# The seam between two layers: the sample tile first, and two chunks of the next layer between the last transposes

## What is computed

```
o = concat(ya, yb) @ w_out_even          # 2048 -> 1024
x1 = x + rmsnorm(o, g_post)
```

```
h = rmsnorm(x1, g_pre)
q, k, v, z, f = split(h @ w_in_odd)      # 4 x 1024 and 8 columns
logf = log_sigmoid(f + b_forget)         # then a running sum over all keys, also over 256 cached rows
```

## Time and profile before

| | |
|---|---|
| median of 3 runs | 1696.01 us |
| the profiled execution | 1696.7 us, its span 1694.9 us |
| TensorE matmuls (PE) busy | 1587.4 us, 94% |
| VectorE (DVE) busy | 809.8 us, 48% |
| ScalarE (ACT) busy | 669.2 us, 39% |
| POOL busy | 440.1 us, 26% |
| mean granted clock of TensorE | 0.976 |

### The profile page before, as it was taken

The page is one execution under the profiler, slowest core; times in us unless marked ns, Lnnn a source line. Parts: engine busy times, 40 slices in busy tenths (PEclk is TensorE's granted clock), DMA queues, the critical chain, the costliest instruction groups (busy, mean ns, idle before and its releaser), DMA issues.

```text
span 1694.9 us, 26649 instructions
## 1 busy us (share of the span) xinstructions
PE 1587.4 (94%) x9562; PEld 1462.9 (86%) x9562; DVE 809.8 (48%) x1753; ACT 669.2 (39%) x1243; POOL 440.1 (26%) x267
## 2 busy tenths in 40 slices
PE   5899999998999999999997999999999999995798
PEld 5899999998998999888886998889889898884576
DVE  5755677664883321336565543443434433342332
ACT  6433333332233332335454344545445445542221
POOL 1113453343212121244442212221213122232000
PEclk9999999999999999999998999999999999997899
DMA  4121213112102111154554444723323342222122
GB/s 143 39 65 56 67 56 97 55 43 67 50 13 66 38 49 37 58 178 150 172 190 88 77 60 42 70 40 63 56 41 70 43 69 41 68 68 75 38 82 75
DMA packets 128740, 121.06 MB, mean 71 GB/s; under 512 B 9706, under 2 KB 112500, under 8 KB 128684
## 3 DMA queue, kind: packets, MB, share of 16 engines
q1 hardware_dynamic: 128684, 120.30, 29.1%
HBM read 101.61 MB, written 18.66 MB: 71 GB/s over the span
## 4 chain that ended last, share of the span: by engine, by line
PE 79%; issue 6%; DVE 6%; ACT 5%; POOL 1%; DMA 1%; SPq 0%; POOLq 0%; ACTq 0%; DVEq 0%
PE PB L720 74%; PE PB L724 5%; DVE NRML L1737 2%; POOL WOL L698 1%; ACT L1239 1%; ACT L1629 1%; ACT SB L1701 1%; ACT WH L1233 0%; DMA XS<-in_x_prompt_dram 0%; ACT NRMH L1233 0%; DMA nf_rows<-NFROW 0%; ACT PT L1233 0%; DVE DTROW L1737 0%; POOL WL L604 0%; DVE XT L1744 0%
## 5 line engine op out<-in xcount | busy, mean ns | idle before, releaser
L720 PE MATMUL PB<-HH,WH 128*128 128x352 f32 x1872 | 620.9, 332 | 14.6 <-ACT XR L1253 6.0
L720 PE MATMUL PB<-HH,WL 128*128 128x352 f32 x1872 | 605.0, 323 | 0.0
L720 PE MATMUL PB<-HL,WH 128*128 128x352 f32 x1872 | 604.4, 323 | 0.0
L720 PEld LDWEIGHTS PB<-HH,WH 128*128 128x128 f32 x1872 | 355.2, 190 | 28.7 <-issue 20.4
L720 PEld LDWEIGHTS PB<-HL,WH 128*128 128x128 f32 x1872 | 355.8, 190 | 0.0
L720 PEld LDWEIGHTS PB<-HH,WL 128*128 128x128 f32 x1872 | 354.5, 189 | 0.0
L604 POOL TENSOR_TENSOR WL<-WRAW,WH 128x1024 fp32r<-128x1024 f32 x82 | 200.5, 2446 | 565.3 <-ACT WH L1233 550.0
L1233 ACT ACTIVATE WH<-WRAW 128x1024 fp32r<-128x1024 f32 x112 | 117.7, 1052 | 26.6 <-DMA WRAW<-in_w_in_even_dram 19.3
L1737 DVE TENSOR_TENSOR Y<-PB,Y 128x128 f32 (+2 forms) x72 | 20.2, 281 | 163.8 <-PE PB L720 163.8
L1701 ACT ACTIVATE SB<-SB,small 128x128 f32<-128x128 f32 (+8 forms) x72 | 53.8, 748 | 81.3 <-DVE small L1741 81.3
L720 PE MATMUL PB<-PT,VTOK 128*128 128x128 f32 (+2 forms) x624 | 82.2, 275 | 0.0
(11 more groups left out here) (290 smaller groups left out, 2453.0 us busy)
## 6 DMA issues: line engine op xcount, KB each, us to landing
WRAW<-in_w_out_even_dram SPq DMA_DIRECT2D x48, 512.0 KB, 3.5
WRAW<-in_w_in_even_dram SPq DMA_DIRECT2D x44, 512.0 KB, 3.8
WRAW<-in_w_in_odd_dram SPq DMA_DIRECT2D x32, 512.0 KB, 8.3
ACSB<-acs_rows SPq DMA_DIRECT2D x16, 528.0 KB, 4.8
NFB<-nf_rows SPq DMA_DIRECT2D x8, 656.0 KB, 3.9
XS<-in_x_prompt_dram SPq DMA_DIRECT2D x8, 512.0 KB, 6.0
XT<-in_x_prompt_dram SPq DMA_DIRECT2D x8, 512.0 KB, 4.8
x_rows<-OG SPq DMA_DIRECT2D x8, 512.0 KB, 5.3
```

Of the source, the lines that this page charges most:

```text
L720: return pe.matmul(out, lhsT, rhs, start=start, stop=stop)
```

## The change

The sample tile is treated first in the closing pass and in the steps behind it: `place` gives the new position of a tile (SMP 6, tile 6 7, tile 7 8), and waits count by it. The interleaving of these steps on ScalarE and VectorE is written out anew. Behind the transposes of tile 6 TensorE does V0 and V1, then the transposes of tile 7, and after F2 goes on with V2. POOL splits the V weights ahead of its wait for `h1_lo` 17. The reads of F0 and F1 on ScalarE stand between the tiles' steps. The transposes of the forget row go from behind Z1 (step 4) to behind Q0 (step 6). The diff, cut to its core:

```diff
+    def place(t):
+        return 6 if t == SMP else t + 1 if t >= 6 else t
+    def h_turns(t):
+        return 2 * t + 2 if t < 6 else 13 if t == SMP else 2 * t + 3
...
 @sync
         def x1_out(b):
-            sp.wait_ge(S("x1"), b + 1)
+            sp.wait_ge(S("x1"), place(b) + 1)
...
-        for b in (6, 7, SMP):
+        for b in (SMP, 6, 7):
             x1_out(b)
         sp.wait_ge(S("h1_lo"), 17)
-        for b in (6, 7, SMP):
+        for b in (SMP, 6, 7):
             sp.wait_ge(S(x1_stored(b)[0]), x1_stored(b)[1])
...
 @gpsimd
         split_low(tile_no(W_F, 1, 0))
+        split_low(tile_no(W_QKVZ + V_, 4, 0))
         pool.wait_ge(S("h1_lo"), 17)
...
-        split_low(tile_no(W_QKVZ + V_, 4, 0))
         split_low(tile_no(W_QKVZ + Z_, 4, 0))
...
 @tensor
-            pair = (2, 3) if b < 3 else (0, 1) if b < 6 else ((4, 5), (6, 7))[b - 6]
+            pair = (2, 3) if b < 3 else (0, 1) if b < 6 else ((2, 3), (4, 5))[b - 6]
...
-        for j, t in enumerate(tiles):
+        for j, t in ((2, SMP), (0, 6), (1, 7)):
             out_step(t, 46, j)
             out_step(t, 47, j).then_inc(S("p_chunk"), 2)
...
         project_chunk(w_f, u_f, 0, HH, HL)
         project_chunk(w_f, u_f, 1, HH, HL)
+        pe.wait_ge(S("o_g"), 14)
+        turn_h1(SMP)
         pe.wait_ge(S("o_g"), 16)
-        pe.wait_ge(S("o_sq"), 16)
         turn_h1(6)
+        project_chunk(w_v, u_v, 0, HH, HL)
+        project_chunk(w_v, u_v, 1, HH, HL)
         pe.wait_ge(S("o_g"), 18)
-        pe.wait_ge(S("o_sq"), 18)
         turn_h1(7)
-        turn_h1(SMP)
         pe.wait_ge(S("h1_lo"), 17)
         project_chunk(w_f, u_f, 2, HH, HL)
...
             for i in range(STEPS):
-                if project:
+                if project and (attend or i >= 2):
                     j = i // 3
                     project_chunk(...)
...
-                if not attend and i == 4:
+                if not attend and i == 6:
                     turn_lrow()
...
 @scalar
+        def read_f(c):
+            act.wait_ge(S("p_chunk"), 3 * W_F + (1, 2, 5)[c])
+            copy(FW[0][:, c * CH:(c + 1) * CH], PB[c][0:HEADS_C, 0:CH]).then_inc(S(f"c_read{c}"), 1)
+        squares(SMP)
+        squares_sample()
         squares(6)
+        root(SMP)
         root(6)
         squares(7)
+        split_high(tile_no(W_QKVZ, 1, 0))
+        squares_x1(SMP)
         squares_x1(6)
+        root_x1(SMP)
+        read_f(0)
         root(7)
-        squares(SMP)
-        split_high(tile_no(W_QKVZ, 1, 0))
         root_x1(6)
+        h1_high(SMP)
         squares_x1(7)
-        squares_sample()
+        read_f(1)
         h1_high(6)
         root_x1(7)
-        root(SMP)
-        squares_x1(SMP)
         h1_high(7)
-        root_x1(SMP)
-        h1_high(SMP)
-        read_chunks(tile_no(W_F, 1, 0), whole(FW[0], HEADS_C), rows=HEADS_C)
+        read_f(2)
         split_high(tile_no(W_F + 2, 1, 0))
         log1p_exp_steps(...)
...
 @vector
+        gained(SMP)
         gained(6)
+        mean(SMP)
         mean(6)
+        residual(SMP)
         gained(7)
         mean(7)
         residual(6)
-        gained(SMP)
-        mean_x1(6)
-        residual(7)
-        normed_x1(6)
-        mean(SMP)
-        mean_x1(7)
-        normed_x1(7)
-        residual(SMP)
-        h1_low(6)
         mean_x1(SMP)
         normed_x1(SMP)
+        residual(7)
+        mean_x1(6)
+        normed_x1(6)
+        h1_low(SMP)
+        mean_x1(7)
+        h1_low(6)
+        normed_x1(7)
         h1_low(7)
-        h1_low(SMP)
```

More of the change, by code:

```diff
@@ L962, in turn_h1 @@
             src = XTT[2 if b == SMP else b % 2]
-            pe.wait_ge(S("xn1"), b + 1)
+            pe.wait_ge(S("xn1"), place(b) + 1)
             if b == SMP:
@@ L1012, in _ @@
         u_f = tile_no(W_F - OE_UNITS, 1, 0)
+        w_v = tile_no(W_QKVZ + V_, 4, 0)
+        u_v = tile_no(W_QKVZ - OE_UNITS + V_, 4, 0)
         pe.wait_ge(S("h1_lo"), 12)
@@ L1152, in turn_steps @@
             for i in range(STEPS):
-                if project:
+                if project and (attend or i >= 2):
                     j = i // 3
                     project_chunk(tile_no(W_QKVZ + j, 4, p), tile_no(W_QKVZ - OE_UNITS + j, 4, p), i % 3, HH, HL)
-                else:
+                if not project:
                     if i == 0:
@@ L1460, in squares @@
             for c in range(2):
-                act.wait_ge(S("p_chunk"), 3 * (W_OE + 16 * (t // 3) + 15) + t % 3 + 1 if t < 6 else 273 + 2 * (t - 5))
+                act.wait_ge(S("p_chunk"), 3 * (W_OE + 16 * (t // 3) + 15) + t % 3 + 1 if t < 6 else 3 * (W_OE + 46) + 2 * (place(t) - 5))
                 bank = PB[PAIRS[t % 4][c]]
@@ L1465, in squares @@
                 else:
-                    wait(act, "o_sq", 2 * t + c)
+                    wait(act, "o_sq", 2 * place(t) + c)
+                    if t == 6:
+                        act.wait_ge(S("s_sq"), 1)
                     act.activation(JUNK[:, c * HALF:(c + 1) * HALF], bank[:, :], ACT.Square,
@@ L1477, in root @@
             rows = sample_rows(t)
-            act.wait_ge(S("o_ms"), t + 1)
+            act.wait_ge(S("o_ms"), place(t) + 1)
             row_root(ORR[0:rows, t:t + 1], OSA[0:rows, t:t + 1], "o_rt")
@@ L1483, in squares_x1 @@
             src = OGT[2 if t == SMP else t % 2]
[L1484 to L1488, removed]
+            act.wait_ge(S("x1"), place(t) + 1)
+            wait(act, "x1_sq", place(t))
+            act.wait_ge(S("o_sq"), 6 * (t // 3) + 4 + 2 * (t % 3 == 2) if t < 6 else 18)
             act.activation(JUNK[0:rows, :], src[0:rows, :], ACT.Square, accum_out=OSX[0:rows, t:t + 1]) \
@@ L1493, in root_x1 @@
             rows = sample_rows(t)
-            act.wait_ge(S("x1_ms"), t + 1)
+            act.wait_ge(S("x1_ms"), place(t) + 1)
             row_root(OSX[0:rows, t:t + 1], OSX[0:rows, t:t + 1], "x1_rt")
@@ L1498, in h1_high @@
             if t == SMP:
-                act.wait_ge(S("h_turn"), 17)
-                copy(HH[:, :, SEQ:TOK], PB[3][:, 0:KT * DEC].rearrange("p (k l) -> p k l", l=DEC)).then_inc(S("h1_hi"), 1)
+                act.wait_ge(S("h_turn"), h_turns(t))
+                copy(HH[:, :, SEQ:TOK], PB[6][:, 0:KT * DEC].rearrange("p (k l) -> p k l", l=DEC)).then_inc(S("h1_hi"), 1)
                 return
-            pair = (2, 3) if t < 3 else (0, 1) if t < 6 else ((4, 5), (6, 7))[t - 6]
+            pair = (2, 3) if t < 3 else (0, 1) if t < 6 else ((2, 3), (4, 5))[t - 6]
             for c in range(2):
-                act.wait_ge(S("h_turn"), 2 * t + c + 1)
+                act.wait_ge(S("h_turn"), h_turns(t) - 1 + c)
                 copy(HH[:, 4 * c:4 * c + 4, t * P:(t + 1) * P],
@@ L2038, in gained @@
                 bank = PB[PAIRS[t % 4][c]]
-                dve.wait_ge(S("o_sq"), 2 * t + c + 1)
+                dve.wait_ge(S("o_sq"), 2 * place(t) + c + 1)
                 if t == SMP:
@@ L2051, in mean @@
                 return
-            dve.wait_ge(S("o_sq"), 2 * t + 2)
+            dve.wait_ge(S("o_sq"), 2 * place(t) + 2)
             ts(OSA[:, t:t + 1], OSA[:, t:t + 1], OSB[:, t:t + 1], D * EPS, ALU.add, ALU.add).then_inc(S("o_ms"), 1)
@@ L2057, in residual @@
             at_ = 2 if t == SMP else t % 2
-            dve.wait_ge(S("o_rt"), t + 1)
+            dve.wait_ge(S("o_rt"), place(t) + 1)
             dve.wait_ge(S(f"x_in{t}"), 32)
             order.fence()
-            dve.wait_ge(S("o_g"), 2 * t + 2)
+            dve.wait_ge(S("o_g"), 2 * place(t) + 2)
             stt(OGT[at_][0:rows, :], OGT[at_][0:rows, :], ORR[0:rows, t:t + 1], XTT[at_][0:rows, :], ALU.mult, ALU.add) \
@@ L2066, in mean_x1 @@
             rows = sample_rows(t)
-            dve.wait_ge(S("x1_sq"), t + 1)
+            dve.wait_ge(S("x1_sq"), place(t) + 1)
             ts(OSX[0:rows, t:t + 1], OSX[0:rows, t:t + 1], D * EPS, None, ALU.add).then_inc(S("x1_ms"), 1)
@@ L2072, in normed_x1 @@
             at_ = 2 if t == SMP else t % 2
-            dve.wait_ge(S("x1_rt"), t + 1)
-            dve.wait_ge(S("x1"), t + 1)
+            dve.wait_ge(S("x1_rt"), place(t) + 1)
+            dve.wait_ge(S("x1"), place(t) + 1)
             stt(XTT[at_][0:rows, :], OGT[at_][0:rows, :], OSX[0:rows, t:t + 1], PREB[0:rows, :], ALU.mult, ALU.mult) \
@@ L2079, in h1_low @@
             if t == SMP:
-                dve.wait_ge(S("h1_hi"), 17)
-                tt(HL[:, :, SEQ:TOK], PB[3][:, 0:KT * DEC].rearrange("p (k l) -> p k l", l=DEC),
+                dve.wait_ge(S("h1_hi"), h_turns(t))
+                tt(HL[:, :, SEQ:TOK], PB[6][:, 0:KT * DEC].rearrange("p (k l) -> p k l", l=DEC),
                    HH[:, :, SEQ:TOK].bitcast(f32), ALU.subtract).then_inc(S("h1_lo"), 1)
                 return
-            pair = (2, 3) if t < 3 else (0, 1) if t < 6 else ((4, 5), (6, 7))[t - 6]
+            pair = (2, 3) if t < 3 else (0, 1) if t < 6 else ((2, 3), (4, 5))[t - 6]
             for c in range(2):
-                dve.wait_ge(S("h1_hi"), 2 * t + c + 1)
+                dve.wait_ge(S("h1_hi"), h_turns(t) - 1 + c)
```

6 lines of the change are left out of this document (3 added, 3 removed).

## The result

The changed kernel takes 1703.6 us (median of 6 runs, 1703.1 to 1705.0); the kernel before takes 1697.3 us in the same comparison (6 runs, 1694.9 to 1699.0). The ratio is 1.0039, 95% interval 1.0029 to 1.0049: slower by 0.4%, with the whole interval beyond the 0.2% (3.4 us) that the prediction took as the least difference a measurement of this kernel can tell. The forecast was 1704.8, range 1698.5 to 1709.5.

What follows compares the result with a forecast made beforehand. The prediction took TensorE, busy 94% of the span, as the bound. Z0 +4.8, half clock in Z0 +2.5 and forget row +1.5 gave +8.8 us: 1705.5 profiled, 1704.8 as median, range 1698.5 to 1709.5.

Steps and rivals of the forecast that it cites:

- the seam: Stretch between the two layers: 8.2 us of TensorE standing still and 2.5 us of half clock, all the change can win.
- T: Moment the last transposed tile is split; 925.4 before, forecast 929.7, or 932.2 with V0 at half clock.
- Z0: First Z chunk, waiting for V0's bank to be read: start at T + 16.3, 948.5 against 943.69, +4.8 us.
- V0's half clock: V0, after a stretch with only short transposes, runs at half clock: 2.5 us, bound 0.
- The tie: POOL's low split of V against VectorE's residual of tile 6, ready within 0.1 us; VectorE taken to go first.
- Rival 3: POOL goes first ahead of VectorE's residual of tile 6: +1.75 us, 1706.6 us; chance 17%.
- Half clock in Z0: Z0 runs at half speed behind TensorE's gap of 8.4 us: +2.5 us, bound 0.
- Forget row: Its transposes move from after Z1 to after Q0, delaying the store of the running sums: +1.5 us.
- Norm sum: Gap ahead of TensorE's first norm sum grows from 1.86 to 3.3 us; possible half clock, 0 to 1.8, left out.
- the list of what would show it: Last transposes at 927 to 930, gap 6 to 9 us ahead of Z0, store 6 to 10 us later.
- Rival 1: Seam filled, V0 read before TensorE finishes V2, Z0 directly behind V2: 1694 us, or 1691.5; chance 8%.
- Rivals 2 and 4: 2: chain to T shorter, 1698.9 us, 12%. 4: V0 runs only after tile 7's transposes, about 1707 us, 4%.

Runs made afterwards that it cites:

- e2: Changed kernel with ScalarE's reads of V0 and V1 moved ahead of the read of F2; 1699.6 us, ratio 1.0011.
- e11: Changed kernel with the store of the running sums issued as soon as they are ready; 1700.9 us, ratio 1.0018.
- e3: Changed kernel with the early Z load and the early reads of V0 and V1; 1699.8 us, ratio 1.0009.
- e9: Changed kernel with early Z load, early reads of V0 and V1, and running sums stored first; 1689.0 us, ratio 0.9952.
- e10: Same edits to the changed kernel as e9, plus tile 7's transposes between V0 and V1; 1690.6 us, ratio 0.9961.
- e1: Changed kernel with SyncE's Z load of head 0 issued early, no longer waiting for T; 1703.3 us, ratio 1.0032.
- e7: Kernel before with the Z load of head 0 issued early, nothing else; 1697.9 us, ratio 1.0000.
- e8: Kernel before with the store of the running sums issued as soon as they are ready; 1693.1 us, ratio 0.9972.
- e6: Kernel before with the sample-first order alone, the change's other moves put back; 1697.4 us, ratio 0.9999.

## Why the prediction was right, point by point

The forecast held by its own mechanism: the seam filled, T came later, and the chain from T to V0's read, hidden before, became the bound of Z0. e2 shows it directly: with V0 and V1 read early and nothing else changed, the wait on V0 is gone, and 4.5 of the 6.3 us with it; e11 shows the second part, the store. The parts, in time of before (1.63 taken off):

- **T.** Forecast 929.7, or 932.2 with V0 at half clock; found 931.1. V0's half clock was mis-sized: six matmuls were slow, about 0.85 us instead of 2.5. The eight transposes of tile 6 were slow as well, 1.94 us against 1.06, some 0.8 us that had been left out. Together that is 1.6 us instead of 2.5, and the transposes of tile 6 start 0.25 us earlier than forecast.
- **POOL and VectorE.** The tie went as taken: the residual of tile 6 started 0.15 us ahead of POOL and took 1.26 us, POOL 3.39 instead of 2.4. Rival 3 is out. It was a close call, 0.06 us in the forecast. Timelines of VectorE and POOL after:

```profile
912.16 1.26 DVE L1760 SCALAR_TENSOR_TENSOR OG<-OG,small,XT 128x1024 f32<-128x1024 f32 x1
...
912.31 3.39 POOL L612 TENSOR_TENSOR WL<-WRAW,WH 128x1024 fp32r<-128x1024 f32 x1 [4.50 <-ACT WH L1245]
```

- **Z0.** Forecast T + 16.3, found T + 15.6: the Z load took 8.4 us from issue to ScalarE's copy, before 9.2 (issued 925.85, copy 935.03). Z0 stands 3.0 us later than before, forecast 4.8 (1.1 of the difference from T, 0.7 from the load). The gap ahead of it is 6.7, forecast 8.4.
- **Half clock in Z0.** Forecast 2.5; 19 matmuls at 0.30 instead of 0.16 us are 2.7. The argument for it was one-sided: "the nearest gaps were each followed by matmuls at half speed" leaves out the gap of 2.66 us, behind which the transposes took 1.06 us, as fast as any.
- **Forget row.** From Z0 to the store's issue 21.3 us, less 2.7 of half clock 18.6, forecast 18.4. The store is issued 7.2 us later than before, forecast 8.8 in sum, 6 to 10 in the list of what would show it.
- **Norm sum.** Gap 3.9, forecast 3.3. The half clock behind it, left out of the sum and bounded at 1.8, came and cost 20 x 0.134 = 2.7 us, more than its bound. This is the term that was missing.
- **V2** waits 0.42 us for the read of F2, which stood in no term; it lies ahead of a longer wait on the same chain and costs nothing here.

The sum: at the start of the norm sum the changed kernel is 7.6 us behind (978.88 − 1.63 − 969.63), where the terms gave 8.8. Z0 took off 1.8; small excesses gave back 0.6, most of it from the store, which took 8.09 us to land instead of 7.71. The half clock behind the norm sum adds the missing 2.7, and 0.9 comes back by the first value store, of which 0.6 are shorter waits at later norm sums. That makes the 9.4 us of the seam.

That the time came out lower is not the mechanism. In the two profiles, 1.6 us are lost ahead of S and 2.6 won back in the tail, in code that is the same; the prediction had no term for either. The medians, 6.3 us apart, lie lower still than the profiles, 8.3 apart. In eleven of the twelve kernels set against the one before, the median moved 0.1 to 3.2 us further down than the seam did, and the cause of that stays open. So it is partly luck that 1704.8 came so near to 1703.6: the forecast difference was 8.8 us, the measured one 6.3, and the kernel before came out 1.3 us higher in this comparison than the 1696.0 that the forecast started from.

Rival 1 (the seam filled, and nothing in its place) names as its condition that V0 is read before TensorE has finished V2. e3 fulfils it, Z0 follows V2 without a gap, and yet the kernel is 2.0 us slower than before and not 2 to 4.5 faster, because the store then holds the norm sum. Only e9 and e10, with the store moved too, bring that rival's gain. Rivals 2 and 4 are excluded by T and by the timeline.

## What to carry to other kernels

When work is moved forward into a gap, ask which later instruction it was covering: here V0 and V1 hid the load, the split and the log steps behind T, and their banks weren't read until all that was done. A freed engine needs its buffers freed by the same amount, so move the reads together with the writes. And when one wait goes and the time stays (e1, e3), read the next wait from the trace before judging the edit: three waits lay here one behind the other (V0's read, POOL's split of the Z weights, the store of the running sums), and of the kernels tried, the changed one came out faster than the one before only with all three taken away (e9 and e10).

## What the runs showed of the hardware that was not expected

**A small store behind large loads.** The running sums (41 KB) took 7.7 us to land before and 8.1 after, issued on SyncE's queue right behind a 512 KB load. In e9, issued 960.28 with that load behind it, ScalarE's copy that waits for it starts 2.1 us later, and so it does in e10 (958.75 and 960.82). The early store also goes ahead of the log row's stores and the key-cache load, and no run varied the size of what stands ahead, so only the order is shown, not which of these transfers held it.

**POOL against VectorE, again and again.** The meeting of e1 repeats in e3, e7, e9 and e10, the first log step waiting 3.97 to 3.98 us each time. In e9 the scan of the forget row meets POOL's next split (954.25 to 956.64) and takes 4.68 us; in the changed kernel, with POOL idle, it took 2.88. This is VectorE's row in e9:

```profile
954.70 4.68 DVE L2184 TENSOR_TENSOR_SCAN NFROW<-ONEROW,LROW 8x1312 f32<-8x1312 f32 x1
```

**The tail.** From the value store of head 6 to the end the thirteen profiles differ by 3.6 us (240.5 to 244.1), although no edit touches that code. There TensorE stands in gaps of up to 5.7 us, most of them behind POOL's splits of the output weights (24 us in all, before and after), and the clock falls at different places of it from profile to profile. The same stretch behind the first of these gaps, 2.2 us long in both, before and after (windows, columns as in the earlier trace rows):

```profile
1520.00:1525.00 5.00, 3.70 (x9) 2.93 (x10) 1.63 (x1) 1.39 (x2) 5.00 (x3) 0.66 0.35 116
```

```profile
1531.00:1536.00 5.00, 3.40 (x18) 2.76 (x18) 1.80 (x4) 1.80 (x3) 5.00 (x3) 1.00 0.31 107
```

Nine matmuls ran at 0.66 in the one, eighteen at 1.00 in the other. The length of the tail goes with these places. Windows counted from the value store of head 6 show the clock falling in the same stretches in before, e7 and e8, whose tails are 242.8 to 243.2 us, and in other stretches, again the same ones, in after, e6 and e9, with 240.5 to 240.8. What sets where the clock falls there was not tried. For a kernel like this it means that two edits of 2 us are hard to rank by their times alone; the stretch that was edited ranks them, S to the first value store.
